# Pooling groups in reverse order, one instruction a level, and group products in four pairs of banks

## The chip, the core and the metric

The kernel runs on one core of a Trainium2 chip. Its engines are TensorE (PE, matmuls into the PSUM banks), VectorE (DVE), ScalarE (ACT), GpSimd (POOL) and SyncE (SP), which issues most transfers. Each has its own queue of instructions and works through it in order; they wait for each other on semaphores. The metric is the time of one execution on the device in microseconds (us).

## The reference

A two-layer decoder trunk runs once for a prompt of 512 positions and for 8 samples of 4 positions, which share the weights. Each layer is a half-step SwiGLU feed-forward, a token mixer and another half-step feed-forward, each followed by a residual and a LayerNorm. The change lies in the mixer of the first layer, a causal pooling:

```
u = x @ w_in                                         # 1024 -> 1024
u_ext = concatenate([prefix, u])                     # 15 rows of history ahead of each sample
for g, w in enumerate((2, 4, 8, 16)):                # four groups of 256 features
    win_sum = sum of u_ext over the last w positions
    pooled = win_sum / min(pos + 1, w) - u           # of the group's 256 features
    outs.append(pooled @ w_grp[g])                   # 256 -> 256
z = concatenate(outs) * scale
mix = z @ w_out                                      # 1024 -> 1024
```

The last 15 rows of `u_ext` are an output too.

## The kernel before

All 544 positions (512 + 32) lie along the columns, and the features on the 128 partitions, in 8 chunks (`DC`). Two halves of 272 columns fill a pair of PSUM banks; there are four pairs, `ps[0]` to `ps[3]`. For precision each matmul of float32 data is made three times: both operands are split into a rounded part ("hi", made by ScalarE) and a remainder ("lo", made by VectorE), and hi x hi, hi x lo and lo x hi are added in PSUM. One output chunk of a 1024 x 1024 weight, a unit below, is 8 steps x 3 x 2 = 48 matmuls of 272 columns. Weights come through two raw tiles (s = 0, 1), which SP loads in order; `round_hi` (ACT, L1352) and `round_lo` (DVE, L1803) make their parts in `whi[s]`/`wlo[s]`. The semaphores `lo_made[s]` and `w_used[s]` say that a weight is ready and that it has been used.

The pooling mixer has three stages, "pin" (x @ w_in), "pgrp" (the group products) and "pout" (z @ w_out):

- **pin.** The first four of the 8 units are made half by half while the LayerNorm ahead still runs (`first_units`, L799): units (0, s) go into `ps[0]` and `ps[1]`, units (1, s) into `ps[2]` and `ps[3]`. Their second half waits step by step for the low part of the normed stream (`x_ready`, L2151). The other four units (i = 2, 3) go into `ps[0]` and `ps[1]`, each after ScalarE has copied the chunk before out of that pair (`u_evac`, L1638 to L1643).
- **windows.** For each chunk c VectorE puts the 15 history rows into the extended chunk `ue[s]` (L2224), then adds level by level (w = 1, 2, 4, 8): a level is one instruction over the prompt's columns (L2230) and one over the samples' (L2232). Group g = c // 2 has g + 1 levels, so the chunks come with 1, 1, 2, 2, 3, 3, 4, 4 levels. Four short instructions make the pooled difference (L2242 to L2249); ScalarE rounds it (L1620), and VectorE makes its low part inside the next chunk's window (L2206, `pooled`). Weight parts of the units to come are made in between.
- **pgrp.** TensorE turns `utail` (the last 47 columns of all chunks) and then makes 8 group products of 12 matmuls, in turn in `ps[0]` and `ps[1]` (L1036 to L1044). A product waits for its two pooled chunks and until the product two before has been read. ScalarE scales each into `zf` and rounds that (L1667, L1669); VectorE makes the low part (L2259, `z_ready`). ScalarE's next read of the same `zf` waits for that.
- **pout.** The first output unit waits for all eight low parts (L1045). Behind it the residual and the next LayerNorm follow, and the feed-forward of up1a.

Of the kernel before, what the change touches and what calls it, by code (L numbers as in the profile page):

```python
# [30 lines left out]
P = 128  # L31
# [58 lines left out]

RBASE = {n: 10 * j for j, n in enumerate(RES)}
# [92 lines left out]
def build(nc, A, O):  # L184
# [9 lines left out]
    with ctx:  # L194
# [320 lines left out]
        def unit_source(stage, s, i):  # L515
# [8 lines left out]
            w = {"pin": w_pin, "pout": w_pout, "kv": w_kv, "q": w_q, "wo": w_o}[stage]  # L524
# [221 lines left out]
        def _(pe):  # L746
            def products(out, s, kt, hi, lo, first=True, last=True, each=None, at=0):


                for k in range(kt):  # L750
                    if each:
                        each(k)
                    for n, (w, a) in enumerate(((whi[s], hi), (whi[s], lo), (wlo[s], hi))):
                        for j in range(2):
                            m = nc.tensor.matmul(out[:, j, 0:HALF], w[:, at + k, :], a(k)[:, j * HALF:(j + 1) * HALF],  # L755
                                                 start=first and k == 0 and n == 0,
                                                 stop=last and k == kt - 1 and n == 2)
                return m
# [40 lines left out]
            def first_units(stage, normed):  # L799
# [25 lines left out]
                for u, k in ((0, 0), (1, 0), (0, 1), (1, 1), (0, 2), (1, 2), (0, 3), (0, 4), (0, 5), (0, 6), (0, 7),  # L825
                             (1, 3), (1, 4), (1, 5), (1, 6), (1, 7)):
# [156 lines left out]
            def linear(stage, hi, lo, evac, normed=None, each=None):  # L983
# [3 lines left out]
                def turn(i, first):  # L987
                    for s in range(2):
# [3 lines left out]
                        products(ps[s], s, KT[stage], hi, lo, each=each if first and s == 0 else None) \  # L992
# [36 lines left out]
            linear("pin", stream_x, stream_xl, lambda s, i: pe.wait_ge(u_evac, 2 * i - 1 + s), "down0b")  # L1029

            pe.wait_ge(u_evac, DC)
            for c in range(DC):
                m = nc.tensor.transpose(pc[0:PAD + SAMP, c // 4, (c % 4) * P:(c % 4 + 1) * P], utail[:, c, :], ident[:])
            m.then_inc(utail_t, 1)

            for g in range(4):  # L1036
                for s in range(2):
                    if g == 0:
                        pe.wait_ge(lo_made[s], USED["pgrp"] + 1)
                    pe.wait_ge(pooled, 2 * g + 2)  # L1040
                    if g >= 1:
                        pe.wait_ge(z_scaled, 2 * g - 1 + s)
                    m = products(ps[s], s, 2, lambda k: phi[:, 2 * g + k, :], lambda k: plo[:, 2 * g + k, :], at=2 * g)
                    m.then_inc(w_used[s] if g == 3 else z_done, 1)  # L1044
            pe.wait_ge(z_ready, DC)  # L1045
            linear("pout", lambda k: zhi[:, k, :], lambda k: zlo[:, k, :],
                   lambda s, i: pe.wait_ge(res_made, RBASE["pout"] + 2 * i - 1 + s))
# [301 lines left out]
        def _(act):  # L1349
# [268 lines left out]
            def pool_hi(c):  # L1618
                act.wait_ge(diff_made, c + 1)
                nc.scalar.activation(phi[:, c, :], (accs, accq)[c % 2], ACT.Copy).then_inc(diff_hi_made, 1)  # L1620

            def pin(i, nxt, j):
                for s in range(2):
                    c = 2 * i + s
                    out = ps[2 + s] if i == 1 else ps[s]
                    if i == 0 and s == 0:
                        round_hi(nxt, 0, j)
                        round_hi(nxt, 1, j)
                    if i > 0:
                        round_hi(nxt, s, j)  # L1630
                    act.wait_ge(w_used[s], USED["pin"] + i + 1)
                    if i >= 1:
                        act.wait_ge(diff_made, 2 * (i - 1) + s + 1)
                        pool_hi(c - 2)
                    else:
                        act.wait_ge(consts_made, 4)
                    samples = ue[s][:, 16 + SEQ:].rearrange("p (b t) -> p b t", t=20)[:, :, 16:20]
                    nc.scalar.activation(ue[s][:, 16:16 + HALF], out[:, 0, 0:HALF], ACT.Copy)  # L1638
                    nc.scalar.activation(ue[s][:, 16 + HALF:16 + SEQ], out[:, 1, 0:SEQ - HALF], ACT.Copy)
                    nc.scalar.activation(samples, out[:, 1, SEQ - HALF:HALF].rearrange("p (b t) -> p b t", t=4),  # L1640
                                         ACT.Copy)
                    nc.scalar.activation(utail[:, c, :], out[:, 1, HALF - PAD - SAMP:HALF], ACT.Copy) \
                        .then_inc(u_evac, 1)  # L1643

            for i in range(UNITS["pin"] - 1):
                pin(i, *coming("pin", i))
                if i >= 1:
                    add_shift("pin", i - 1)
            pin(UNITS["pin"] - 1, "pgrp", 0)
            pool_hi(DC - 2)  # L1650
            pool_hi(DC - 1)
# [4 lines left out]


            for c in range(DC):
                s = c % 2
                if c < DC - 2:  # L1660
                    act.wait_ge(z_done, c + 1)
                else:
                    act.wait_ge(w_used[s], USED["pgrp"] + 1)
# [938 lines left out]
```

## Time and profile before

| | us |
|---|---|
| median of 3 runs | 2211.88 |
| lowest and highest of them | 2200.86 to 2218.66 |
| profiled execution, span from first to last instruction (the page gives no other time for it) | 2210.1 |
| TensorE busy in it | 2089.8 (95%) |
| VectorE, ScalarE, GpSimd busy | 1423.9, 871.4, 227.9 |

The page gives the busy time of each engine and the groups of instructions that cost most. What the rows further down add is an order in time: the timeline of one engine, with the idle time ahead of an instruction and the instruction that ended it, the chain of waits (the work that ended last, followed back from the end), and the busy time of all engines in chosen stretches, with the clock that TensorE was granted (1.00 is 2.4 GHz, 0.50 is 1.2 GHz). The pooling mixer lies from about 425 to 547 us of the span.

### The profile page before, as it was taken

To read this page: it belongs to the slowest core of one execution; us is meant where nothing else is said; L and a number is where in the kernel's file an instruction comes from. 1 tells how busy PE (TensorE), PEld (TensorE's weight loads), DVE (VectorE), ACT (ScalarE), POOL (GpSimd) and SP (SyncE) were. 2 spreads that over 40 slices of the span, in tenths; PEclk is the share of its full clock that TensorE was granted. 3 is DMA by queue.
4 is the path that set the end of the run, shared out by engine and by line. 5 is a ranking of instruction groups with operands and counts; after the bars stand their busy time and mean duration, and the time that the engine had idled before them with its cause. 6 is when DMAs were issued, how large, how long until landed. Compare 5 with 4: busy or idle time off the path is not lost.

```text
span 2210.1 us, 43553 instructions
## 1 busy us (share of the span) xinstructions
PE 2089.8 (95%) x16575; PEld 2016.3 (91%) x16575; DVE 1423.9 (64%) x2388; ACT 871.4 (39%) x1529; POOL 227.9 (10%) x265
## 2 busy tenths in 40 slices
PE   7999999989899999999999999999978789999998
PEld 7999999989899999999999999988866588999997
DVE  3483795674786498378639836266746377838955
ACT  3342453353543255254415524222234345514533
POOL 0000002304100000410000031111012140000022
PEclk9999999999999999999999999999989899999998
DMA  4242433222233233324423333656576422333331
GB/s 140 64 134 84 124 116 107 78 61 77 66 98 102 78 97 94 91 64 147 124 88 96 102 88 108 203 181 224 187 252 219 137 77 86 93 89 95 95 102 54
DMA packets 381501, 249.80 MB, mean 113 GB/s; under 512 B 10422, under 2 KB 363038, under 8 KB 381326
## 3 DMA queue, kind: packets, MB, share of 16 engines
q1 hardware_dynamic: 371271, 210.00, 32.0%
q0 software_dynamic: 10096, 37.94, 5.0%
q8 instruction: 93, 1.52, 0.3%
q14 instruction: 41, 0.34, 0.1%
HBM read 230.63 MB, written 22.35 MB: 114 GB/s over the span
## 4 chain that ended last, share of the span: by engine, by line
PE 73%; DVE 11%; DMA 7%; issue 4%; ACT 3%; SPq 1%; POOL 1%; DVEq 0%; ACTq 0%; POOLq 0%
PE pair L755 33%; PE pair L884 27%; PE pair L794 5%; DMA t_w_raw<-in_attn_w_kv 4%; PE pair L1012 2%; DMA t_w_raw<-in_ffn_w 2%; DVE t_w_seven L1938 2%; PE pair L1238 1%; DVE t_w_sum L1933 1%; PE pair L767 1%; DVE t_w_lo L1816 1%; ACT t_w_hi L1367 1%; DVE t_u_sum L2230 1%; DVE t_stream L2144 1%; DVE t_work L2136 1%
## 5 line engine op out<-in xcount | busy, mean ns | idle before, releaser
L884 PE MATMUL pair<-t_x_diff_hi,t_w_seven 128*128 128x272 f32 x1960 | 409.9, 289 | 0.0
L1816 DVE TENSOR_TENSOR t_w_lo<-t_w_raw,t_w_hi 128x1024 fp32r<-128x1024 f32 (+2 forms) x152 | 232.8, 1532 | 203.3 <-ACT t_w_hi L1367 198.6
L1367 ACT ACTIVATE t_w_hi<-t_w_raw 128x1024 fp32r<-128x1024 f32 (+2 forms) x152 | 177.2, 1170 | 462.8 <-PE pair L755 383.7
L884 PEld LDWEIGHTS pair<-t_x_diff_hi,t_w_seven 128*128 128x128 f32 x1960 | 320.3, 188 | 0.0
L755 PE MATMUL pair<-t_h_lo,t_w_hi 128*128 128x272 f32 x1232 | 254.8, 288 | 0.0
L755 PE MATMUL pair<-t_h_hi,t_w_lo 128*128 128x272 f32 x1232 | 254.6, 288 | 0.0
L755 PE MATMUL pair<-t_h_hi,t_w_hi 128*128 128x272 f32 x1232 | 254.5, 288 | 0.0
L884 PE MATMUL pair<-t_x_hi,t_w_seven 128*128 128x272 f32 x1120 | 240.7, 294 | 10.8 <-DVE t_c L1942 9.5
L884 PE MATMUL pair<-t_x_diff_lo,t_w_seven 128*128 128x272 f32 x840 | 241.7, 288 | 0.0
L884 PEld LDWEIGHTS pair<-t_x_hi,t_w_seven 128*128 128x128 f32 x1120 | 184.5, 188 | 23.1 <-issue 12.4
L755 PEld LDWEIGHTS pair<-t_h_hi,t_w_lo 128*128 128x128 f32 x1232 | 193.2, 188 | 0.0
L755 PEld LDWEIGHTS pair<-t_h_hi,t_w_hi 128*128 128x128 f32 x1232 | 193.2, 188 | 0.0
L755 PEld LDWEIGHTS pair<-t_h_lo,t_w_hi 128*128 128x128 f32 x1232 | 193.0, 188 | 0.0
L1438 ACT ACTIVATE t_w_seven<-t_w_sum 128x512 fp32r<-128x512 f32 x210 | 124.6, 622 | 113.7 <-PE pair L884 78.6
L884 PE MATMUL pair<-t_x_lo,t_w_seven 128*128 128x272 f32 x560 | 161.5, 288 | 0.0
L884 PEld LDWEIGHTS pair<-t_x_diff_lo,t_w_seven 128*128 128x128 f32 x840 | 158.4, 189 | 0.0
L2455 POOL MEMSET t_work<- 128x544 f32 x6 | 3.3, 555 | 1374.0 <-DVE t_stream L2086 1374.0
L1938 DVE TENSOR_TENSOR t_w_seven<-t_w_sum,t_w_seven 128x512 fp32r<-128x512 f32 x210 | 143.2, 682 | 0.2
L1438 ACT ACTIVATE t_s_hi<-t_w_sum 128x512 fp32r<-128x512 f32 x70 | 44.3, 633 | 241.5 <-DVE t_w_sum L1933 229.7
L755 PE MATMUL pair<-t_x_hi,t_w_hi 128*128 128x272 f32 x576 | 123.8, 297 | 15.1 <-DVE t_w_lo L1816 10.4
L755 PE MATMUL pair<-t_x_lo,t_w_hi 128*128 128x272 f32 x576 | 123.0, 296 | 0.0
L755 PE MATMUL pair<-t_x_hi,t_w_lo 128*128 128x272 f32 x576 | 122.3, 294 | 0.0
(320 smaller groups left out, 4898.1 us busy)
## 6 DMA issues: line engine op xcount, KB each, us to landing
t_w_raw<-in_ffn_w SPq DMA_DIRECT2D x280, 256.0 KB, 3.1
t_w_raw<-in_ffn_w SPq DMA_DIRECT2D x64, 704.0 KB, 4.6
t_w_raw<-in_ffn_w SPq DMA_DIRECT2D x36, 512.0 KB, 3.8
t_cached<-in_cache_kv_w POOLq DMA_DIRECT2D x16, 1024.0 KB, 9.3
t_cached_v<-in_cache_kv_w POOLq DMA_DIRECT2D x16, 1024.0 KB, 10.8
t_w_raw<-in_attn_w_kv SPq DMA_DIRECT2D x24, 512.0 KB, 8.2
t_w_raw<-in_attn_w_q SPq DMA_DIRECT2D x12, 512.0 KB, 3.8
scratch_bias_rows<-scratch_bias_row SPq DMA_DIRECT2D x12, 384.0 KB
```

Of the source, the lines that this page charges most:

```text
L755: m = nc.tensor.matmul(out[:, j, 0:HALF], w[:, at + k, :], a(k)[:, j * HALF:(j + 1) * HALF], start=first and k == 0 and n == 0, stop=last ...
L767: return nc.tensor.matmul(out[:, j, 0:HALF], invd[:], a[:, hcols(j)], start=first, stop=not first)
L794: m = nc.tensor.matmul(ps[2 * u + s][:, j, 0:HALF], w[:, k, :], a[:, k, hcols(j)], start=k == 0 and n == 0, stop=k == DC - 1 and n == 2)
L884: m = nc.tensor.matmul(out[:, 0:HALF], w[:, k, :], b, start=start and k == 0 and j == 0, stop=k == 3 and j == 2, skip_group_check=not start)
L1012: m = nc.tensor.matmul(ps[s][:, j, 0:HALF], w[:, k, :], a(k)[:, hcols(j)], start=k == 0 and n == 0, stop=k == KT[stage] - 1 and n == 2)
L1238: m = nc.tensor.matmul(pd[32 * n:32 * n + 32, 0, :], p_b[:, n, t, :], v_c0[n] if t == 0 else v_c[n // 2][:, 4 * (n % 2) + t - 1, :], start ...
L1367: nc.scalar.activation(whi[s][:, 0:KT[stage], :], raw[s][:, 0:KT[stage], :], ACT.Copy) \
L1438: nc.scalar.activation(seven_hi[n][:], src, ACT.Copy).then_inc(seven_hi_made, 1)
L1816: nc.vector.tensor_tensor(wlo[s][:, 0:k, :], raw[s][:, 0:k, :], whi[s][:, 0:k, :].bitcast(F32), ALU.subtract).then_inc(lo_made[s], 1)
L1933: nc.vector.tensor_tensor(w_sum[m][:], a, b, op).then_inc(w_sum_made, 1)
L1938: nc.vector.tensor_tensor(seven_lo[n][:], src, seven_hi[n][:].bitcast(F32), ALU.subtract) \
L2136: step.add(nc.vector.reciprocal(rstd[:, hcols(j)], rstd[:, hcols(j)]))
```

## The change

The chunks go through pin and the windows in reverse: position o stands for chunk `chunk_of(o)`, 6, 7, 4, 5, 2, 3, 0, 1, so the four-level windows come first, and SP reads the columns of w_in in that order. The half-made units are finished one after the other, not interleaved. Units 2 go into `ps[0]`/`ps[1]` and units 3 into `ps[2]`/`ps[3]`. A level is one instruction over the prompt's and the samples' columns together; ScalarE copies the history rows, ahead of the chunk's other copies, and GpSimd fills `ue` with zeros beforehand. The 8 group products go round the four pairs of banks, in the order of `Z_ORDER` = (6, 4, 7, 5, 2, 3, 0, 1). ScalarE scales and rounds a product in one instruction from PSUM, and VectorE makes its low part from PSUM as well; `zf` is gone. The first output unit takes its eight steps in `Z_ORDER`, each as its low part is there, and turns `utail` ahead of its last step.

```diff
+def chunk_of(o):
+    return 2 * (3 - o // 2) + o % 2
+Z_ORDER = (6, 4, 7, 5, 2, 3, 0, 1)
...
+            if stage == "pin":
+                return w_pin[:, :, bass.ds(-2 * P * i + (6 + s) * P, P)]
...
+                if stage == "pin":
+                    second_half = [(u, k) for u in range(2) for k in range(DC)]
+                for u, k in second_half:
                     pe.wait_ge(x_ready, ready + DC + k + 1)
...
-            linear("pin", stream_x, stream_xl, lambda s, i: pe.wait_ge(u_evac, 2 * i - 1 + s), "down0b")
...
+            first_units("pin", "down0b")
+            for i in (2, 3):
+                for n in range(2):
+                    pe.wait_ge(lo_made[n], USED["pin"] + i + 1)
+                    pe.wait_ge(u_evac, n + 1 if i == 2 else n + 3)
+                    products(ps[n if i == 2 else 2 + n], n, DC, stream_x, stream_xl).then_inc(w_used[n], 1)
+            def grouped(n, g, w):
+                pe.wait_ge(pooled, 2 * (3 - g) + 2)
+                return products(ps[n % 4], w, 2, lambda k: phi[:, 2 * g + k, :], lambda k: plo[:, 2 * g + k, :], at=2 * g)
+            for n, g in ((0, 3), (1, 2)):
+                if n == 0:
+                    pe.wait_ge(lo_made[0], USED["pgrp"] + 1)
+                pe.wait_ge(u_evac, 5 + n)
+                grouped(n, g, 0).then_inc(z_done, 1)
+            for n, g in ((2, 3), (3, 2)):
+                if n == 2:
+                    pe.wait_ge(lo_made[1], USED["pgrp"] + 1)
+                pe.wait_ge(u_evac, 5 + n)
+                grouped(n, g, 1).then_inc(z_done, 1)
+            for n in (4, 5):
+                pe.wait_ge(z_ready, n - 3)
+                grouped(n, 1, n - 4).then_inc(z_done, 1)
+            for n in (6, 7):
+                pe.wait_ge(z_ready, n - 3)
+                grouped(n, 0, n - 6).then_inc(w_used[n - 6], 1)
+            def pout_first(k):
+                if k == Z_ORDER[0]:
+                    pe.wait_ge(z_ready, 5)
+                pe.wait_ge(z_ready, Z_ORDER.index(k) + 1)
+                if k == Z_ORDER[-1]:
...
             linear("pout", lambda k: zhi[:, k, :], lambda k: zlo[:, k, :],
+                   lambda s, i: pe.wait_ge(res_made, RBASE["pout"] + 2 * i - 1 + s), each=pout_first, order=Z_ORDER)
...
+            def evacuated(o):
+                i, n, c = o // 2, o % 2, chunk_of(o)
+                out = ps[2 + n] if i % 2 else ps[n]
+                samples = ue[n][:, 16 + SEQ:].rearrange("p (b t) -> p b t", t=20)
+                if o >= 2:
+                    act.wait_ge(diff_made, o - 1)
+                elif o == 0:
+                    act.wait_ge(consts_made, 4)
+                nc.scalar.activation(samples[:, :, 1:16], hist[:, c, :].rearrange("p (b t) -> p b t", t=PAD), ACT.Copy)
+                act.wait_ge(w_used[n], USED["pin"] + i + 1)
...
+            def scaled_hi(n):
+                c = Z_ORDER[n]
+                if n < 6:
+                    act.wait_ge(z_done, n + 1)
+                else:
+                    act.wait_ge(w_used[n - 6], USED["pgrp"] + 1)
+                nc.scalar.activation(split(zhi[:, c, :]), halves(ps[n % 4]), ACT.Copy, scale=par[:, PS + c:PS + c + 1]) \
+                    .then_inc(z_scaled, 1)
...
+            round_hi("pin", 1, 3)
+            pool_hi(2)
+            evacuated(4)
+            pool_hi(3)
+            evacuated(5)
+            round_hi("pgrp", 0, 0)
+            pool_hi(4)
+            evacuated(6)
+            round_hi("pgrp", 1, 0)
+            pool_hi(5)
+            evacuated(7)
...
+            for n in range(4, 7):
+                scaled_hi(n)
+            round_hi("pout", 0, 0)
+            scaled_hi(7)
+            round_hi("pout", 1, 0)
...
+            def window(o):
+                n, g = o % 2, chunk_of(o) // 2
...
+                for level in range(g + 1):
+                    dst = us[level % 2]
+                    step.add(nc.vector.tensor_tensor(dst[:, 2 * w - 1:end], src[:, 2 * w - 1:end], src[:, w - 1:end - w],
+                                                     ALU.add))
+                    if o == 0 and level == 0:
+                        round_lo("pin", 0, 2)
...
+                if o in (2, 3):
+                    round_lo("pin", o - 2, 3)
+                if o in (5, 6):
+                    round_lo("pgrp", o - 5, 0)
+                if o:
+                    pool_lo(o - 1)
...
+                if o == 0:
+                    round_lo("pin", 1, 2)
+            def scaled_lo(n):
+                c = Z_ORDER[n]
+                dve.wait_ge(z_scaled, n + 1)
+                nc.vector.scalar_tensor_tensor(out=split(zlo[:, c, :]), in0=halves(ps[n % 4]),
+                                               scalar=par[:, PS + c:PS + c + 1], in1=split(zhi[:, c, :]).bitcast(F32),
+                                               op0=ALU.mult, op1=ALU.subtract).then_inc(z_ready, 1)
...
             centre("down0b")
...
+            for s in range(2):
+                nc.gpsimd.memset(ue[s][:], 0.0).then_inc(consts_made, 1)
```

Three places of the instruction order show what moves. In these rows a number behind a name tells buffers apart (`pair0` is `ps[0]`), and in brackets stand the semaphores that an instruction waits for.

VectorE at the start of the windows, before:

```order
L1816 TENSOR_TENSOR t_w_lo0<-t_w_raw0,t_w_hi0 128x1024 [waits hi_made0,consts_in]
L1816 TENSOR_TENSOR t_w_lo1<-t_w_raw1,t_w_hi1 128x1024 [waits hi_made1]
L2224 COPY t_u_ext0<-t_history 128x8x15 [waits state_evacuated]
L2230 TENSOR_TENSOR t_u_sum0<-t_u_ext0 128x527 [waits u_evacuated,dve_step]
L2232 TENSOR_TENSOR t_u_sum0<-t_u_ext0 128x8x18
L2242 TENSOR_TENSOR t_u_sum1<-t_u_sum0,t_inv_count 128x16 [waits dve_step]
L2243 SCALAR_TENSOR_TENSOR t_work<-t_u_sum0,t_u_ext0 128x496
L2245 SCALAR_TENSOR_TENSOR t_work<-t_u_sum0,t_u_ext0 128x32
L2249 TENSOR_TENSOR t_work<-t_u_sum1,t_u_ext0 128x16 [waits dve_step]
```

and now:

```order
L2265 TENSOR_TENSOR t_u_sum0<-t_u_ext0 128x687 [waits u_evacuated,consts_in]
L1862 TENSOR_TENSOR t_w_lo0<-t_w_raw0,t_w_hi0 128x1024 [waits hi_made0]
L2265 TENSOR_TENSOR t_u_sum1<-t_u_sum0 128x685 [waits dve_step]
L2265 TENSOR_TENSOR t_u_sum0<-t_u_sum1 128x681 [waits dve_step]
L2265 TENSOR_TENSOR t_u_sum1<-t_u_sum0 128x673 [waits dve_step]
L2281 TENSOR_TENSOR t_u_sum0<-t_u_sum1,t_inv_count 128x16 [waits dve_step]
L2282 SCALAR_TENSOR_TENSOR t_work<-t_u_sum1,t_u_ext0 128x496
L2284 SCALAR_TENSOR_TENSOR t_work<-t_u_sum1,t_u_ext0 128x32
L2288 TENSOR_TENSOR t_work<-t_u_sum0,t_u_ext0 128x16 [waits dve_step]
L1862 TENSOR_TENSOR t_w_lo1<-t_w_raw1,t_w_hi1 128x1024 [waits hi_made1]
```

The first chunk's first level stands ahead of both weight parts instead of behind them, it is one instruction, and the copy of the history has left VectorE; the first chunk has four levels instead of one.

VectorE between the last windows and the output weights, before:

```order
L2249 TENSOR_TENSOR t_work<-t_u_sum0,t_u_ext1 128x16 [waits dve_step]
L2206 TENSOR_TENSOR t_pool_lo<-t_work,t_pool_hi 128x544 [waits pool_hi_made]
L2259 TENSOR_TENSOR t_z_lo<-t_elementwise,t_z_hi 128x544 [waits z_scaled] x7
L1816 TENSOR_TENSOR t_w_lo0<-t_w_raw0,t_w_hi0 128x1024 [waits hi_made0]
L2259 TENSOR_TENSOR t_z_lo<-t_elementwise,t_z_hi 128x544 [waits z_scaled]
L1816 TENSOR_TENSOR t_w_lo1<-t_w_raw1,t_w_hi1 128x1024 [waits hi_made1]
```

and now:

```order
L2295 SCALAR_TENSOR_TENSOR t_z_lo<-pair0,t_params,t_z_hi 128x544 [waits z_scaled]
L2295 SCALAR_TENSOR_TENSOR t_z_lo<-pair1,t_params,t_z_hi 128x544 [waits z_scaled]
L2265 TENSOR_TENSOR t_u_sum0<-t_u_ext1 128x687 [waits u_evacuated,pool_diff_made]
...
L2288 TENSOR_TENSOR t_work<-t_u_sum1,t_u_ext1 128x16 [waits dve_step]
L2295 SCALAR_TENSOR_TENSOR t_z_lo<-pair2,t_params,t_z_hi 128x544 [waits z_scaled]
L2251 TENSOR_TENSOR t_pool_lo<-t_work,t_pool_hi 128x544 [waits pool_hi_made]
L2295 SCALAR_TENSOR_TENSOR t_z_lo<-pair3,t_params,t_z_hi 128x544 [waits z_scaled]
...
L1862 TENSOR_TENSOR t_w_lo0<-t_w_raw0,t_w_hi0 128x1024 [waits hi_made0]
L2295 SCALAR_TENSOR_TENSOR t_z_lo<-pair2,t_params,t_z_hi 128x544 [waits z_scaled]
...
L1862 TENSOR_TENSOR t_w_lo1<-t_w_raw1,t_w_hi1 128x1024 [waits hi_made1]
```

Three of the scaled low parts (`t_z_lo`) moved ahead of the last low pooled part (`t_pool_lo`), and all eight read a pair of banks instead of `zf` in SBUF (`t_elementwise`).

TensorE, the first matmul of each group product and what stands next to it, before:

```order
L1033 MATMUL pair2<-t_ident,t_u_tail 47x128 [waits u_evacuated]
L755 MATMUL pair0<-t_pool_hi,t_w_hi0 128x272 [waits pooled,lo_made0]
...
L755 MATMUL pair1<-t_pool_hi,t_w_hi1 128x272 [waits pooled,lo_made1]
...
L755 MATMUL pair0<-t_pool_hi,t_w_hi0 128x272 [waits z_scaled,pooled]
...
L755 MATMUL pair1<-t_pool_hi,t_w_hi1 128x272 [waits z_scaled,pooled]
...
L755 MATMUL pair0<-t_z_hi,t_w_hi0 128x272 [waits lo_made0,z_parts_ready]
```

and now:

```order
L762 MATMUL pair0<-t_pool_hi,t_w_hi0 128x272 [waits pooled,u_evacuated,lo_made0]
...
L762 MATMUL pair1<-t_pool_hi,t_w_hi0 128x272 [waits pooled,u_evacuated]
...
L762 MATMUL pair2<-t_pool_hi,t_w_hi1 128x272 [waits pooled,u_evacuated,lo_made1]
...
L762 MATMUL pair3<-t_pool_hi,t_w_hi1 128x272 [waits pooled,u_evacuated]
...
L762 MATMUL pair0<-t_pool_hi,t_w_hi0 128x272 [waits pooled,z_parts_ready]
...
L762 MATMUL pair1<-t_pool_hi,t_w_hi1 128x272 [waits pooled,z_parts_ready]
...
L762 MATMUL pair0<-t_z_hi,t_w_hi0 128x272 [waits z_parts_ready,lo_made0]
...
L762 MATMUL pair0<-t_z_hi,t_w_hi0 128x272 [waits z_parts_ready]
...
L1075 MATMUL pair2<-t_ident,t_u_tail 47x128 [waits z_parts_ready]
```

The third to eighth product waited for `z_scaled` of the pair that it writes, two products before it; now the first four wait for pooled chunks and banks alone, and only the last four for a low part (`z_parts_ready`). The turning of `utail` moved from ahead of the group products into the first output unit.

## Rows read from the trace of the kernel before

**Rows 1.** The page, busy time of TensorE: us, share of the span, instructions.

```profile
PE 2089.8 (95%) x16575; PEld 2016.3 (91%) x16575; DVE 1423.9 (64%) x2388; ACT 871.4 (39%) x1529; POOL 227.9 (10%) x265
```

**Rows 2.** Busy time in stretches: us, us long, busy us (x) of each engine, PEclk, DMA.

```profile
454.00:482.00 28.00, 24.67 (x197) 24.24 (x196) 27.35 (x70) 17.51 (x43) 0.00 (x0) 1.00 0.27 76
482.00:491.00 9.00, 2.35 (x17) 1.92 (x15) 6.62 (x17) 3.24 (x7) 1.10 (x2) 0.85 0.20 59
```

**Rows 3.** Chain of waits, pooling stage: start, us, what.

```profile
487.99 0.66 ACT t_pool_hi L1620
...
491.04 6.61 PE pair L755 x36
```

**Rows 4.** VectorE in time, a window of four levels: start, us, instruction, [idle before it and its releaser].

```profile
476.22 0.21 DVE L2224 COPY t_u_ext<-t_history 128x120 f32<-128x120 f32 x1
476.47 0.71 DVE L2230 TENSOR_TENSOR t_u_sum<-t_u_ext 128x527 f32<-128x527 f32 x1
477.09 0.30 DVE L2232 TENSOR_TENSOR t_u_sum<-t_u_ext 128x144 f32<-128x144 f32 x1
...
479.28 0.69 DVE L2230 TENSOR_TENSOR t_u_sum<-t_u_sum 128x513 f32<-128x513 f32 x1
...
479.99 0.72 DVE L2206 TENSOR_TENSOR t_pool_lo<-t_work,t_pool_hi 128x544 fp32r<-128x544 f32 x1
480.62 0.17 DVE L2242 TENSOR_TENSOR t_u_sum<-t_u_sum,t_inv_count 128x16 f32<-128x16 f32 x1
...
481.48 1.22 DVE L1816 TENSOR_TENSOR t_w_lo<-t_w_raw,t_w_hi 128x1024 fp32r<-128x1024 f32 x1
```

**Rows 5.** VectorE in time, the ends of its chain.

```profile
444.93 0.50 DVE L2151 SCALAR_TENSOR_TENSOR t_x_lo<-t_stream,t_params,t_x_hi 128x272 fp32r<-128x272 f32 x1 [0.18 <-ACT t_x_hi L1570]
...
449.52 2.36 DVE L1816 TENSOR_TENSOR t_w_lo<-t_w_raw,t_w_hi 128x1024 fp32r<-128x1024 f32 x2 [4.05 <-ACT t_w_hi L1367]
...
488.68 0.72 DVE L2206 TENSOR_TENSOR t_pool_lo<-t_work,t_pool_hi 128x544 fp32r<-128x544 f32 x1 [0.72 <-ACT t_pool_hi L1620]
```

**Rows 6.** TensorE in time: second half of the projection, two pauses, two output products.

```profile
440.21 0.29 PE L794 MATMUL pair<-t_x_hi,t_w_hi 128*128 128x272 f32 x1
...
480.00 1.07 PE L1033 MATMUL pair<-t_ident,t_u_tail 128*47 128x128 f32 x8 [2.48 <-ACT t_u_tail L1642]
...
505.47 0.82 PE L755 MATMUL pair<-t_z_hi,t_w_hi 128*128 128x272 f32 x2 [2.66 <-DVE t_z_lo L2259]
...
513.07 0.41 PE L755 MATMUL pair<-t_z_hi,t_w_hi 128*128 128x272 f32 x2
```

**Rows 7.** Chain of waits, a stage at the full clock.

```profile
167.31 66.38 PE pair L755 x528
```

**Rows 8.** ScalarE in time: the first copy out of PSUM, the second chunk's.

```profile
450.27 0.38 ACT L1638 ACTIVATE t_u_ext<-pair 128x272 f32<-128x272 f32 x1
...
450.96 0.42 ACT L1638 ACTIVATE t_u_ext<-pair 128x272 f32<-128x272 f32 x1
```

**Rows 9.** Groups by line and form: xcount, busy us, mean ns, idle before.

```profile
L1367 ACT ACTIVATE t_w_hi<-t_w_raw 128x1024 fp32r<-128x1024 f32 x8 | 8.3, 1054 | 10.8 <-PE pair L755 7.4 <-PE pair L794 3.5
L2259 DVE TENSOR_TENSOR t_z_lo<-t_elementwise,t_z_hi 128x544 fp32r<-128x544 f32 x8 | 5.8, 725 | 8.8 <-ACT t_z_hi L1669 8.7
L1667 ACT ACTIVATE t_elementwise<-pair,t_params 128x544 f32<-128x544 f32 x8 | 5.7, 708 | 3.2 <-PE pair L755 3.0
```

**Rows 10.** VectorE in time, the same operands from PSUM.

```profile
513.26 0.73 DVE L2086 SCALAR_TENSOR_TENSOR t_stream<-pair,t_stream 128x544 f32<-128x544 f32 x1 [6.40 <-PE pair L755]
```

**Rows 11.** Busy time and PEclk in single microseconds.

```profile
506.00:507.00 1.00, 1.00 (x7) 1.00 (x6) 0.86 (x1) 0.00 (x0) 0.00 (x0) 0.50 0.92 272
509.00:510.00 1.00, 1.00 (x10) 1.00 (x10) 0.00 (x0) 0.00 (x0) 0.00 (x0) 1.00 1.00 302
```

**Rows 12.** GpSimd in time: a fill of 544 columns.

```profile
514.05 0.55 POOL L2455 MEMSET t_work<- 128x544 f32 x1 [22.86 <-DVE t_stream L2086]
```

**Rows 13.** Transfers, 440 to 520 us: issues, KB each, median us to landing.

```profile
t_w_raw<-in_pool_w_out SPq DMA_DIRECT2D x5, 512.0 KB, 4.1
```

More of the change, by code:

```diff
@@ L746, in _, with products @@
         def _(pe):
-            def products(out, s, kt, hi, lo, first=True, last=True, each=None, at=0):
-                for k in range(kt):
+            def products(out, s, kt, hi, lo, each=None, at=0, order=None):
+                order = order or range(kt)
+                for k in order:
                     if each:
@@ L755, in products @@
                             m = nc.tensor.matmul(out[:, j, 0:HALF], w[:, at + k, :], a(k)[:, j * HALF:(j + 1) * HALF],
-                                                 start=first and k == 0 and n == 0,
-                                                 stop=last and k == kt - 1 and n == 2)
+                                                 start=k == order[0] and n == 0,
+                                                 stop=k == order[-1] and n == 2)
                 return m
@@ L981, in down, with linear @@
                 linear(stage, lambda k: hhi[:, k, :], lambda k: hlo[:, k, :], evac, each=each)
-            def linear(stage, hi, lo, evac, normed=None, each=None):
+            def linear(stage, hi, lo, evac, normed=None, each=None, order=None):
                 base = USED[stage]
@@ L991, in turn @@
                             evac(s, reused(stage, i))
-                        products(ps[s], s, KT[stage], hi, lo, each=each if first and s == 0 else None) \
+                        products(ps[s], s, KT[stage], hi, lo, each=each if first and s == 0 else None, order=order) \
                             .then_inc(w_used[s], 1)
@@ L1615, in _ @@
             norm("down0b", 0)
[L1618 to L1643, printed above, removed]
@@ new lines, in scaled_lo @@
+            def scaled_lo(n):
[4 more added lines that the diff above has]
+                                               op0=ALU.mult, op1=ALU.subtract).then_inc(z_ready, 1)
+            dve.wait_ge(consts_in, 32)
+            for o in range(7):
+                window(o)
@@ L2264, in _ @@
+            scaled_lo(0)
+            scaled_lo(1)
+            window(7)
+            scaled_lo(2)
+            pool_lo(7)
+            for n in range(3, 6):
+                scaled_lo(n)
+            round_lo("pout", 0, 0)
+            scaled_lo(6)
+            scaled_lo(7)
+            round_lo("pout", 1, 0)
             residual_pair("pout")
```

155 lines of the change are left out of this document (60 added, 95 removed).

## The prediction

> **What bounds the kernel now.** I read the page first: TensorE is busy for 95% of the span [rows 1], so a change in one stage is worth the TensorE time that this stage leaves empty, and no more. The busy time by stretches then shows where it is empty: from 454 to 482 us 3.3 of 28.0 us, and from 482 to 491 us, where the pooling windows end, 6.65 of 9.0 [rows 2]. The chain of waits says who is waited for there: ScalarE's high part of the last pooled chunk at 487.99, and only from 491.04 on the group products that follow [rows 3]. VectorE in time shows the reason: four-level windows end the stage, and its chain of one instruction after another runs from 449.52 to 488.68 + 0.72 = 489.40 [rows 4, 5]. TensorE in time: it waited 2.48 us for the last `u_tail`, and 2.66 us before the first output product at 505.47 [rows 6]. So the stage is bound by VectorE until 489.4, then by the ping-pong of six group products on two banks, product, scale, part, next product, for 505.47 - 489.40 = 16.07 us.
>
> **The prices.** A full-rate matmul of 272 columns costs 66.38 / 528 = 0.1257 us [rows 7]; a unit of 48 is 6.03, a group product of 12 is 1.51. On VectorE I count from start to start, which is the duration less 0.09 where nothing is waited for (476.47 to 477.09 for 0.71), and the duration plus about 0.04 where the next needs the result (476.22 + 0.21 to 476.47) [rows 4]. The new level instruction of up to 687 columns is not in the trace. Between 144 columns (0.30) and 527 (0.71) a column costs 0.00107 us, so 687 cost 0.71 + 160 x 0.00107 = 0.88 [rows 4]: 0.92 with a wait behind it, 0.79 without. Its bounds: 0.71, a row with fewer columns, and 1.01, the two that it replaces (0.71 + 0.30). I take 0.88, nearest to the larger row. The four instructions that close a window cost 481.48 - 480.62 = 0.86, a low pooled part 0.63, a weight's low part 1.22 - 0.08 = 1.14 [rows 4].
>
> The scaled low part, a SCALAR_TENSOR_TENSOR of 544 columns that reads PSUM, stands in the trace as a residual: 0.73, against 0.725 for the subtraction from SBUF that it replaces [rows 9, 10]. I take 0.64 from start to start, as 0.63 above. The Trainium skill, VectorE: DVE Perf Modes, section on the TRN2 errata, prices the fixed part of a VectorE instruction at 120 cycles from PSUM and 58 from SBUF, at 0.96 GHz. By that each would cost 0.065 us more, and the three ahead of the last pooled part 0.2 us together, for a gain of 15.6 instead of the 15.8 below; the rows do not show it.
>
> **The change, part by part.** *Head.* The first unit's second half now runs by itself: eight steps of six matmuls from 440.21 [rows 6], each 0.75 and held by a low part of the stream, the last of which ends at 444.93 + 0.50 = 445.43 [rows 5]. Unit 0 ends at about 446.2; before, three steps of unit 1 stood between, and 11 x 0.75 give 448.5. ScalarE copies the chunk at once (four copies, 450.96 - 450.27 = 0.69 [rows 8]) and rounds the next weight behind it, not ahead of it, so VectorE's first level starts at about 446.9. Unit 1 still ends at 452.25, since the number of matmuls is the same.
>
> *VectorE from there to the last low pooled part.* Windows without the parts: with four levels 3 x 0.92 + 0.79 + 0.87 = 4.42; three 3.50, two 2.58, one 1.66; two of each are 24.3. Eight pooled parts 5.0, six weight parts 6.8, three scaled parts 1.9: 38.1 in all, and I add 0.9 for some 15 hops between engines. It ends at 446.9 + 39.0 = 485.9, 3.5 us before 489.4. Of these 3.5, 2.6 are the early start, 2.0 the eight history copies (476.47 - 476.22 = 0.25 each [rows 4]) that go to ScalarE, some 0.8 the merged levels and a shorter last wait; the three scaled parts, now ahead of the end, take 1.9 back.
>
> *TensorE beside it.* Units 2 to 5 (four of 48) run from 452.25 to 458.3, 464.3, 470.3 and 476.4, if their weights' low parts are there. In VectorE's order these end at 449.0, 453.8, 462.7 and 468.1: the least margin is 1.6 us, at the third (464.3 - 462.7). The two group weights end at 475.9 and 479.4. Four products into four pairs of banks run from 476.4 to 482.5 and wait for nothing but the second weight; two more, behind the low parts of the first two, to 485.5; the last two wait for the last pooled part and run from 485.95 to 488.97.
>
> *Tail.* Behind 485.9 there is now: two products 3.02, with the seventh's high part (0.71) and the first output weight's rounding (1.05) and low part (1.22) behind the first of them [rows 4, 9]: 487.5 + 0.6 + 1.05 + 1.25 = 490.4. TensorE starts the output products at 490.45, after a pause of 1.5 us, instead of at 505.47: 15.0 us earlier, 3.5 of it before the last pooled part and 11.5 behind.
>
> *First output unit.* It took 513.07 - 505.47 = 7.60 us [rows 6], 1.57 above 6.03, since the granted clock was 0.50 there [rows 11]. It was low after a pause of 2.66 us and had stayed at 1.00 through one of 2.48 [rows 2, 6, 11], so I expect it to stay after 1.5. The `u_tail` transposes now stand inside this unit: eight, 0.83 us. Net gain 0.74. **Sum: 15.0 + 0.74 = 15.8 us at the end of that unit.** Behind it TensorE's order is as before.
>
> *At nothing:* the history copies on ScalarE, bounded by 0.25 each (VectorE's), stand ahead of chunks for which VectorE is 1.7 us late or more, except the first two, where ScalarE waits for TensorE; without that cover they cost 8 x 0.25 = 2.0. GpSimd's two fills of 688 columns (0.55 for 544 [rows 12], so 0.7 each) end some 5 us before the first copy. One wide copy less per scaled chunk on ScalarE is inside the 11.5. Transfers: 4.1 us from issue to landing [rows 13]; the output weights are issued when the group weights' low parts are made, at 475.9 and 479.4, and wanted at 488.1 and 489.7, so they are not late. SP's queue keeps its order; only the columns that it reads are reversed. GpSimd's two stores of `u_tok` and ScalarE's two copies for them move into the first output unit, where both engines wait for TensorE.
>
> **Against the runs.** The sum is made on the profiled execution, of which the page gives the span, 2210.1, and no other time. The median 2211.88 lies 1.8 above it. I take the difference over to the median: 2211.88 - 15.8 = **2196 us**, 0.7% faster. More is not to be had: from 452.25 the stage holds 4 x 6.03 + 8 x 1.51 + 0.83 + 6.03 = 43.1 us of matmuls, which would end at 495.3, and 513.07 - 495.3 = 17.8 is the most.
>
> **Rivals.** *Ring waits, 12%.* TensorE waits for a weight's low part, VectorE for ScalarE's high part, ScalarE at the head of its queue for TensorE to let go of the old weight. Margins are 1.6 us at the third late weight and about 0.5 and 0 at the group weights; if each of four such turns comes 2 us late, 8 us are lost: 2204. For it: level instructions at their upper bound make VectorE 20 x 0.13 = 2.6 late. Against: VectorE waited 0.72 us in its chain before [rows 5].
>
> *The clock falls, slower, 3%.* The products now run in batches of 1.5 us on four pairs of banks with small pauses, then pause 1.5 us. If the clock went to its lower level, 1.2 GHz, at 476 and stayed there through the output products, 12.1 + 288 x 0.1257 = 48.3 us of matmuls would double: 2211.88 - 15.8 + 48.3 = 2244. It decides from 15.8 us of doubled work on. Against it: 1.00 through a pause of 2.48 us, and the return to 1.00 inside the first output unit [rows 2, 6, 11]. The Trainium skill, TensorE: Matmul & The Clock Gate, section on psum-queue depth-cycling, says that such cycling through banks, with TensorE idle for a moment between groups, makes the clock fall and rise again. In this stage of the trace it fell only behind pauses of 2.66 us and more.
>
> *Gained and given back, 5%.* A wait behind the stage eats the gain, 2212: the one transfer that could is an output weight, with 3 us to spare.
>
> The forecast has 80%. It covers gains of 10 (levels at 1.01, the clock low for the first output unit, 1 us of hops) to 17.8: 2194 to 2202. The three runs of before lie 11.0 below and 6.8 above their median, so a median of after may be read 10 us off. **Range 2183 to 2208**, which takes in the ring. Within 1% means 22 us, about what a measurement of this kernel can tell from no change; no case gains that much, so "faster by over 1%" is left to the scatter, about one in five of the forecast: 0.17. Slower by over 1% is the clock's case: 0.03. The rest is 0.80.
>
> **What would show it.** In the profile after: the first level at about 447, the last low pooled part ending near 486, no pause of TensorE over 2 us from 452 to the output products, these beginning near 490, and the granted clock 1.00 throughout. It is wrong if TensorE pauses inside the four late units, if the level rows are over 1.0 us, or if a wait of that size comes up behind the first output unit.

## The result: 0.8% shorter, the stage as forecast

The changed kernel took 2192.36 us (median of four runs, 2189.58 to 2195.15) beside 2212.68 (2200.86 to 2218.66) of the kernel before: ratio 0.9921, interval 0.9898 to 0.9945. The forecast was 2196, range 2183 to 2208; the time lies in it, 3.6 us below the forecast, and 0.8% shorter by the ratio, inside the 1% that held 0.80 of the chances. The profiled execution after has a span of 2193.5 us and took 2195.15.

The page after, TensorE's busy time, answers to [rows 1]: the work is the same, and 3.0 us less is counted (the second execution of before counts 2086.8 too).

```profile
PE 2086.8 (95%) x16575; PEld 2014.1 (92%) x16575; DVE 1421.7 (65%) x2358; ACT 867.4 (40%) x1529; POOL 228.8 (10%) x267
```

Busy time in stretches after, in the columns of [rows 2]:

```profile
454.00:482.00 28.00, 28.00 (x225) 27.86 (x224) 27.62 (x55) 15.53 (x41) 0.00 (x0) 1.00 0.27 77
482.00:491.00 9.00, 7.07 (x55) 6.67 (x54) 6.58 (x9) 4.48 (x7) 0.00 (x0) 1.00 0.18 55
```

The 3.33 us that TensorE left empty from 454 to 482 are gone, 6.65 us of the next nine are now 1.93, and the granted clock is 1.00 in both. TensorE's waits over the stage (444 to 506 us; in total, times, longest), the kernel before first:

```profile
PE pair L755 <- ACT t_z_hi L1669: 6.5, 1, 6.5
PE pair L755 <- DVE t_z_lo L2259: 2.7, 1, 2.7
PE pair L1033 <- ACT t_u_tail L1642: 2.5, 1, 2.5
PE pair L755 <- DVE t_w_lo L1816: 1.0, 2, 0.8
```

and after:

```profile
PE pair L762 <- DVE t_w_lo L1862: 1.5, 1, 1.5
PE pair L762 <- DVE t_pool_lo L2251: 0.4, 1, 0.4
```

The chain of waits after, the pooling stage (start, us, what), answers to [rows 3, 5, 6]:

```profile
426.19 16.77 PE pair L801 x132
...
443.93 0.88 DVE t_u_sum L2265
...
482.07 0.73 DVE t_pool_lo L2251
482.94 1.76 PE pair L762 x12
...
485.33 1.06 ACT t_w_hi L1400
486.42 1.24 DVE t_w_lo L1862
487.70 5.51 PE pair L762 x42
493.21 0.87 PE pair L1075 x8
```

It reads as forecast: VectorE's levels to the last low pooled part, two group products, the first output weight, the output products. But both executions have to be put on one start. Ahead of the change, where the code is equal, the second execution already led: the products of the projection's second unit begin in the chain at 429.43 before and at 426.19 after. Their first product stands 0.37 us ahead of that; TensorE in time, before and after:

```profile
429.06 0.49 PE L794 MATMUL pair<-t_x_hi,t_w_hi 128*128 128x272 f32 x1
```

```profile
425.82 0.49 PE L801 MATMUL pair<-t_x_hi,t_w_hi 128*128 128x272 f32 x1
```

**D** is the time from that first product to the first output product (505.47 before [rows 6], 487.70 after): **76.41 us before, 61.88 after, 14.53 less**, where 15.0 were forecast.

### The profile page after: what moved, and what is told of

It reads as the page before. It is cut to its first block, busy times and chain, and to the rows that moved or that the text cites. A ratio compares the mean times of both kernels' runs of the same rounds, so it can differ in the third digit from the quotient of the medians.

```text
span 2193.5 us, 43507 instructions
## 1 busy us (share of the span) xinstructions
PE 2086.8 (95%) x16575; PEld 2014.1 (92%) x16575; DVE 1421.7 (65%) x2358; ACT 867.4 (40%) x1529; POOL 228.8 (10%) x267
## 4 chain that ended last, share of the span: by engine, by line
PE 73%; DVE 11%; DMA 6%; issue 4%; ACT 3%; SPq 1%; POOL 1%; DVEq 0%; ACTq 0%; POOLq 0%
PE pair L762 33%; PE pair L894 27%; PE pair L801 5%; DMA t_w_raw<-in_attn_w_kv 3%; PE pair L1022 2%; DMA t_w_raw<-in_ffn_w 2%; DVE t_w_seven L1984 2%; DVE t_w_lo L1862 1%; PE pair L1271 1%; DVE t_w_sum L1979 1%; PE pair L774 1%; DVE t_u_sum L2265 1%; ACT t_w_hi L1400 1%; DVE t_stream L2190 1%; DVE t_u L1988 1%
## 5 line engine op out<-in xcount | busy, mean ns | idle before, releaser
L894 PE MATMUL pair<-t_x_hi,t_w_seven 128*128 128x272 f32 x1120 | 240.7, 295 | 11.2 <-DVE t_c L1988 9.9
```

The lines of the kernel that those rows point to most:

```text
L894: m = nc.tensor.matmul(out[:, 0:HALF], w[:, k, :], b, start=start and k == 0 and j == 0, stop=k == 3 and j == 2, skip_group_check=not start)
```

## The experiments

All are read by D, since single runs of this kernel spread by over 10 us and D by much less. "Pooled" is the end of the last low pooled part, counted from the chain's start of that unit (429.43 before, 426.19 after).

| kernel | D, us | pooled | what is different |
|---|---|---|---|
| before, twice | 76.41, 77.05 | 59.97, 60.02 | |
| change, twice | 61.88, 61.93 | 56.60, 56.66 | |
| head alone | 72.64 | 55.37 | tail as before |
| tail alone | 69.24 | 63.74 | head as before, natural order |
| u1 | 64.00 | 58.73 | interleaved first units |
| u3 | 64.21 | 58.95 | two instructions a level, copies on VectorE |
| u4 | 62.92 | 56.86 | parts through SBUF |
| u2 | 67.30 | 59.15 | two pairs of banks |
| u6 | 65.82 | 55.37 | scaled parts behind the windows |
| u5 | 69.24 | 62.66 | natural order |
| n1 | 65.72 | 59.14 | natural order, weights' parts later |
| b1 | 61.37 | 56.64 | a shorter pause ahead of pout |

**The two kernels once more (no edit).**

> The kernel before, once more, for its scatter. D is the time from the first product of pin's second unit (it stands right behind the sums of the norm) to the first product of pout: 76.41 us in the first profile of before, 61.88 in the first of the changed kernel. Theory (the stage's gain of 14.5 us belongs to the code, the 3.2 us by which the changed kernel led ahead of the stage do not): D is 76.4 +- 0.4 again, while the start of that first product may lie anywhere in 425 to 430. Rival (part of the 14.5 is the scatter of one execution): D is off by 1 us or more.

> The changed kernel, once more. Theory: D is 61.9 +- 0.4; the norm sums behind pout take 3.4 us or 6.2 us, whichever clock the execution meets, since nothing there was changed; total about 20 us below before with an interval that holds 15. Rival (the change itself lowers the clock behind pout): they take 6.2 us again here and in every variant that starts pout early, and 3.4 only with the tail of before.

D came out 77.05 and 61.93. The change repeats; before missed its 0.4 us, and stayed short of the rival's 1. Of the 0.64 us, 0.59 lie in the three group products behind TensorE's longest pause: their 36 matmuls took 7.20 us, 6.61 the first time [rows 3], and 4.53 (36 x 0.1257) would be the full clock. The unit that D counts from began anywhere from 423.99 to 430.17 us in the traces of this study, so the lead of 3.2 us was scatter. The change again: 2193.11 us beside 2210.94, ratio 0.9917 (0.9899 to 0.9934). The norm sums behind pout separate the two executions of the same code. Chain of waits, first profile after:

```profile
544.23 1.05 PE pair L801 x3
545.28 1.81 PE pair L774 x4
...
550.41 19.20 PE pair L801 x153
```

and the second one:

```profile
545.35 0.65 PE pair L801 x3
546.00 0.92 PE pair L774 x4
...
548.75 19.20 PE pair L801 x153
```

From the start of these three matmuls to the chain that follows it is 6.18 us in the one, at a granted clock of 0.54 in the mean, and 3.40 in the other, at 1.00. Over the variants it fell on either kind: 5.07 us with the tail of before (head alone), 3.40 in b1, which has the tail of the change. So the rival that the change lowers the clock there falls. In the first profile it gave back 2.78 of the stage's gain.

**Head alone, tail alone.** Tail alone has the natural order, of which this is the core, and the edits of u1 and u3 below:

```diff
 def chunk_of(o):
-    return 2 * (3 - o // 2) + o % 2
+    return o
-Z_ORDER = (6, 4, 7, 5, 2, 3, 0, 1)
+Z_ORDER = (0, 2, 1, 3, 4, 5, 6, 7)
```

> The tail alone: chunks in natural order, the first two units' second halves interleaved as before, two instructions a level and the history copies on VectorE; group products on four pairs of banks and parts straight from PSUM, scaled parts between the windows, as in the change. Theory (head and tail add up, the reverse order by itself gives nothing): 2.3 us lost by the interleaving and 2.4 by VectorE's longer chain, D = 66.6 (65.5 to 68), total about 10 us below before. Rival (the reverse order, long windows first, is what lets six of eight products run before the last pooled part): D = 70 or more.

Head alone has the edits of u2, u4 and u6 below, together.

> The head alone: reverse order, the first unit finished by itself, one instruction a level, history copies on ScalarE as in the change; group products on two pairs of banks, scaled through SBUF by two ScalarE instructions, all scaled parts behind the last pooled part, as before. Theory: the last low pooled part ends 2.2 us earlier than in the change (no scaled part ahead of it), the ring of before's 16.1 us follows: D = 70 (69 to 72), total about 6 us below before. Rival (the reverse order alone brings most): D below 66. Rival (the head is worth nothing without the tail): D above 74.

Tail alone: D = 69.24, between theory and rival, so missed; 2204.72 us, ratio 0.9975 (0.9959 to 0.9991). Head alone: D = 72.64, just over the range; 2206.12 us, ratio 0.9973 (0.9957 to 0.9989). Apart they gain 3.8 to 4.4 and 7.2 to 7.8 us of D, 10.9 to 12.2 of 14.5 to 15.1: the parts don't simply add up. Head alone shows the old ring; TensorE's waits over the stage:

```profile
PE pair L762 <- issue: 6.6, 1, 6.6
PE pair L762 <- DVE t_w_lo L1862: 2.4, 1, 2.4
PE pair L762 <- DVE t_z_lo L2295: 1.0, 4, 0.3
```

**One part undone: the order.** u5 has the natural order and nothing else: the two lines above, the unit's columns from the front, and in the group products

```diff
+                g = 3 - g
-                pe.wait_ge(pooled, 2 * (3 - g) + 2)
+                pe.wait_ge(pooled, 2 * g + 2)
```

> The change with the chunks in natural order (short windows first), all else as in the change. D is 61.9 in the change; the tail alone had 69.2, of which 2.3 + 2.4 were expected of its interleaving and its longer VectorE chain, and 2.6 stay over. Theory (the 2.6 are the order: with short windows first VectorE waits between chunks, and the long ones end the stage): D = 64.5 (63.5 to 66). Rival (the order is worth nothing, the two undone head parts cost more than their sum): D = 62 (61.5 to 62.7).

D = 69.24, 7.4 us above the change and the same as in tail alone: theory and rival both missed. 2201.38 us, ratio 0.9958 (0.9936 to 0.998) to before. VectorE in time shows where it stands still:

```profile
456.87 1.22 DVE L1863 TENSOR_TENSOR t_w_lo<-t_w_raw,t_w_hi 128x1024 fp32r<-128x1024 f32 x1 [3.34 <-ACT t_w_hi L1401]
...
462.87 1.22 DVE L1863 TENSOR_TENSOR t_w_lo<-t_w_raw,t_w_hi 128x1024 fp32r<-128x1024 f32 x1 [1.47 <-ACT t_w_hi L1401]
```

The low part of the next weight stands in the middle of a window in VectorE's order; ScalarE can round that weight only when TensorE has let go of the old one, every 6.0 us. Behind a short window VectorE is there early and waits, and the rest of the window with it. With the long windows first it is never early: in the change VectorE shows no such wait from its first level (443.93) to 486.42. With the natural order the head parts, 4.4 us in the change, are worth little. For these two weights VectorE waits 4.8 us in u5 and 2.0 in tail alone, and the last pooled part comes 1.1 us earlier in u5. That D is the same looks like chance: the next product met a lower clock in u5, which took the 1.1 us back. The chain of tail alone, then of u5:

```profile
488.24 1.99 PE pair L762 x12
```

```profile
489.35 3.07 PE pair L762 x12
```

n1 is u5 with the parts of pin's last two weights one window later, and their roundings on ScalarE one chunk later:

```diff
-                if o in (2, 3):
-                    round_lo("pin", o - 2, 3)
+                if o in (3, 4):
+                    round_lo("pin", o - 3, 3)
```

> The change in natural order again, with the roundings of pin's last two weights and their low parts one window later on ScalarE and VectorE. In natural order as first run (D = 69.2, 7.3 us above the change) VectorE stood still 3.34 and 1.47 us in the windows of chunks 2 and 3, behind low parts of weights that ScalarE could round only when TensorE had let go of the old ones. Theory (the reverse order gains because long windows cover those weights): the two pauses go or shrink below 1 us, the last low pooled part ends 59 to 60 us after the second unit's products begin instead of 62.7, D = 64.8 (64 to 66.3). Rival (the order matters at the end: long windows last hold the stage up whatever stands between the first): D = 68 or more.

D = 65.72, pooled 59.14, both in the ranges: the first two waits for a weight's part are gone, one of 0.56 us is left, beside 0.96 and 0.62 for the high parts of the first two pooled chunks. 2198.26 us, ratio 0.9937 (0.992 to 0.9953). So 3.5 of the order's 7.4 us were those waits. The other 3.8 are 2.5 by which the last pooled part is still later and 1.3 of clock: TensorE paused 3.1 us for it, and the next product (12 matmuls) then took 3.07 us, against 1.76 in the change. The first row is the chain of n1, the second its busy time and clock (0.50):

```profile
486.66 3.07 PE pair L762 x12
```

```profile
486.60:489.70 3.10, 3.04 (x13) 3.07 (x14) 1.99 (x3) 0.36 (x1) 0.00 (x0) 0.50 0.00 0
```

**One part undone: the head.** u1 leaves out two lines:

```diff
-                if stage == "pin":
-                    second_half = [(u, k) for u in range(2) for k in range(DC)]
```

> The change with the second halves of pin's first two units interleaved as before. Theory (VectorE's chain is the bound from the first chunk on, so its later start shows in full): the first level 2.3 us later, D = 64.2 (63.8 to 64.6). Rival (VectorE waits for chunks later on anyway, the start is hidden): D = 62 (61.5 to 62.5).

u3 copies the history on VectorE, not on ScalarE, and adds each level in two instructions:

```diff
+                step.add(nc.vector.tensor_copy(tail(e)[:, :, 1:16],
+                                               hist[:, chunk_of(o), :].rearrange("p (b t) -> p b t", t=PAD)))
...
-                    step.add(nc.vector.tensor_tensor(dst[:, 2 * w - 1:end], src[:, 2 * w - 1:end], src[:, w - 1:end - w],
-                                                     ALU.add))
+                    nc.vector.tensor_tensor(dst[:, 2 * w - 1:16 + SEQ], src[:, 2 * w - 1:16 + SEQ],
+                                            src[:, w - 1:16 + SEQ - w], ALU.add)
+                    step.add(nc.vector.tensor_tensor(tail(dst)[:, :, 2 * w:20], tail(src)[:, :, 2 * w:20],
+                                                     tail(src)[:, :, w:20 - w], ALU.add))
```

> The change with two instructions a level and the history copies on VectorE. Theory (20 merged levels bring at most 0.8, eight copies of 0.25 us 2.0, all of it on VectorE's chain): D = 64.3 (63.7 to 64.9). Rival (both are hidden by chunks that come late): D = 62 (61.5 to 62.5).

D = 64.00 and 64.21, both in the range: 2.1 us for the start of the chain, 2.3 for its length, all of it on the path. (One run each, 2195.87 and 2194.67 us, which alone would say nothing.)

**One part undone: the tail.** In u2 `n % 4` becomes `n % 2` for the products and both parts, and the waits of products 2 and 3, of 4 to 7, and of pout become

```diff
-                pe.wait_ge(u_evac, 5 + n)
+                pe.wait_ge(z_ready, n - 1)
...
-                pe.wait_ge(z_ready, n - 3)
+                pe.wait_ge(z_ready, n - 1)
...
-                    pe.wait_ge(z_ready, 5)
+                    pe.wait_ge(z_ready, 7)
```

> The change with the group products on two pairs of banks (each product waits until the part of the product two earlier is read, and pout until both pairs are free); scaled parts between the windows and straight from PSUM stay. Theory (each turn of the ring costs a product, a high and a low part, some 3 us, but most turns lie beside windows): D = 65 (64 to 67). Rival (the four pairs carry the tail's gain): D = 68 or more. Rival (they are worth nothing): D below 62.5.

u4 scales into SBUF and rounds from there; the low part is a subtraction from SBUF:

```diff
...
+                step.add(nc.scalar.activation(split(zf[:]), halves(ps[n % 4]), ACT.Copy, scale=par[:, PS + c:PS + c + 1]))
+                act.wait_ge(act_step, step.value())
+                nc.scalar.activation(zhi[:, c, :], zf[:], ACT.Copy).then_inc(z_scaled, 1)
```

> The change with the scaled chunks going through SBUF: two ScalarE instructions of 0.70 and 0.66 us each instead of one, VectorE subtracting from SBUF. Theory (ScalarE has idle time between the windows, so only the parts behind the last pooled part show): D = 63.1 (62.6 to 64.5); VectorE's low part takes 0.72 instead of 0.72 to 0.77 us. Rival (parts straight from PSUM carry the tail's gain): D = 66 or more.

u6 on ScalarE; on VectorE the low parts move alike:

```diff
-            scaled_hi(0)
-            scaled_hi(1)
             pool_hi(6)
-            scaled_hi(2)
-            scaled_hi(3)
             pool_hi(7)
-            for n in range(4, 7):
+            for n in range(7):
                 scaled_hi(n)
```

> The change with all scaled parts behind the last pooled part, as before (four pairs of banks and parts straight from PSUM stay). Theory: the last low pooled part ends 2.2 us earlier (three scaled parts fewer ahead of it), but products 5 to 8 wait for the parts one after another: D = 63 (62.4 to 64). Rival (the place of the parts among the windows is what the tail's gain is made of): D = 66 or more.

u2: D = 67.30, 0.3 over the range, 0.7 short of the rival's. u4: 62.92, in the range. u6: 65.82, missed, 0.2 short of the rival's. Both misses have the clock in them, which their expectations left out. u2's chain:

```profile
480.98 4.79 PE pair L762 x24
...
488.56 3.29 PE pair L762 x24
...
495.59 4.47 PE pair L762 x34
```

and its busy time and clock:

```profile
478.00:481.00 3.00, 0.82 (x8) 0.63 (x6) 3.00 (x8) 2.29 (x6) 0.00 (x0) 1.00 0.39 114
481.00:483.00 2.00, 2.00 (x11) 2.00 (x12) 2.00 (x5) 0.00 (x0) 0.00 (x0) 0.64 0.47 138
```

The ring makes TensorE pause 2.2 us, and the two products behind it take 4.79 us instead of 3.02. Then ScalarE, held by the scaled part of the second of them, comes late to the last pooled part (pooled 2.5 us later). In u6 the pooled part comes 1.2 us earlier, but TensorE pauses 2.8 us ahead of the fifth product, and three products take 6.33 us instead of 4.53 (chain of u6):

```profile
482.15 6.33 PE pair L762 x36
```

**A shorter pause ahead of pout.** In the change ScalarE scales the seventh chunk and rounds the first output weight after it, while TensorE waits 1.5 us. b1 turns that round, and the `u_tail` transposes go ahead of pout, into `ps[1]`:

```diff
-            for n in range(4, 7):
-                scaled_hi(n)
+            scaled_hi(4)
+            scaled_hi(5)
             round_hi("pout", 0, 0)
+            scaled_hi(6)
             scaled_hi(7)
```

> The change, with pout's first weight rounded ahead of the seventh scaled part, and the tail transposes moved from the first output unit into the pause ahead of it (into the second pair of banks). Theory (the pause of 1.5 us ahead of pout is ScalarE's order and nothing else): D = 61.3 (60.9 to 61.5), the first output unit 0.87 us shorter, 1.5 us gained at its end; total 1.5 us below the change, less than a comparison of this kernel can show. Rival (the pause is filled, but a later wait comes up, for the seventh and eighth scaled parts or the second weight): the unit's end is not earlier by more than 0.5 us.

D = 61.37, in the range; TensorE waits in all 0.4 us in the stage (its waits, 444 to 506 us):

```profile
PE pair L762 <- DVE t_pool_lo L2255: 0.4, 1, 0.4
```

From the first output product to the end of the norm sums behind pout b1 takes 59.04 us, against 59.94 in the second profile of the change, so 1.4 us are gained in all, as expected. The total, 2194.27 us and ratio 0.9936 (0.9913 to 0.9958) to before, can't show that: b1 is better in the profile, and not shown to be faster than the change.

## Why the prediction was right, step by step

- **Head, 3.5 us.** Pooled came 3.37 us earlier (59.97 to 56.60). Its terms: 2.6 for the early start, 2.1 by u1; 2.8 for copies and levels, 2.3 by u3; 1.9 given back for three scaled parts ahead of the end, 1.2 by u6. That is 3.2 of the 3.37. Only two of the three parts cost time: the third runs while ScalarE rounds the last pooled chunk, where VectorE waits 0.72 us in u6. A merged level took 0.88 us as priced. The price of the scaled low part was low: from start to start two of them took 1.39 / 2 = 0.70, where 0.64 was taken. VectorE in time, after: two scaled parts, then for comparison one pooled part of the same size from SBUF and an instruction of the same kind from SBUF:

```profile
477.60 1.47 DVE L2295 SCALAR_TENSOR_TENSOR t_z_lo<-pair,t_params,t_z_hi 128x544 fp32r<-128x544 f32 x2
...
479.77 0.72 DVE L2251 TENSOR_TENSOR t_pool_lo<-t_work,t_pool_hi 128x544 fp32r<-128x544 f32 x1
...
480.49 0.66 DVE L2282 SCALAR_TENSOR_TENSOR t_work<-t_u_sum,t_u_ext 128x496 f32<-128x496 f32 x1
```

  Behind the last of these rows the next instruction starts at 481.08, so 496 columns took 0.59 from start to start, and 544 would take 0.64 (an estimate with 0.00107 a column); the kind of instruction is not what makes 0.70. The Trainium skill, VectorE: DVE Perf Modes, section on the TRN2 errata, would have 0.065 us more for a source in PSUM; the trace agrees, with 0.06.
- **TensorE beside it.** No pause from 454 to 482, as forecast, and the waits of TensorE shown with the result name none of the late weights.
- **Tail, 11.5 us.** From the last low pooled part to pout it was 16.07 us before and is 487.70 - 482.80 = 4.90: 11.2 less. The pause ahead of pout is 1.51, forecast 1.5. Not all of the 16.07 was the ping-pong, as the prediction has it: 2.1 us (6.61 less 4.53 [rows 3]; 2.7 in the second execution) were the low clock of three products behind the pause of 6.5 us, which went with the pause; the size of the step stays the same by it. And the step took the gain as one sum and said nothing of what carries it. Undone alone, the order costs 7.4 us, the two pairs 5.4, the late parts 3.9, the way through SBUF 1.0; with the head's 4.4 that is 22 for a gain of 14.5. Each of the larger ones opens a pause of TensorE of over 2 us and then pays for the clock as well, so the price of one part depends on the others.
- **First output unit, 0.74.** The clock stayed at 1.00, and the transposes took 0.87 inside it. From the first output product to the end of the norm sums behind pout it was 60.48 us before (565.95 - 505.47) and 59.94 in the second profile of the change: 0.54.
- **Sum, 15.8.** From the second unit's chain start to the end of the norm sums behind pout it is 565.95 - 429.43 = 136.52 us before and 550.41 - 426.19 = 124.22 after, or 121.44 without the 2.78 of the low clock: 15.1 less. In the second pair it is 137.22 and 121.50: 15.7 less. The medians differ by 20.3 and, in the larger comparison, 17.8 us. The other 2 to 5 us need not be the change's, and that the median lies 3.6 us below the forecast says nothing: ahead of the stage traces differ by 6.2 us, and behind those norm sums by up to 7.4 (1639.8 to 1647.2 us to the end of the span). The interval of the second comparison, 14.6 to 22.3 us, holds the stage's gain. The chain of waits before, both ends of the 136.52 us:

```profile
429.43 18.85 PE pair L794 x150
...
565.95 19.20 PE pair L794 x153
```

- **Rivals.** The ring waits did not come (one wait of 0.4 us). The clock fell in neither profile from 454 us to pout, so the forecast held, but one of its grounds did not: the pause of 2.48 us that had kept 1.00 was followed by 0.50 in the second execution of before, and in tail alone the clock fell behind 1.9 us. That the clock stays up behind 1.5 us rests on the five profiles that have this pause (the change twice, u1, u3, u6). What the first profile gave back behind pout was not a wait, as the third rival has it, but the clock, in one execution of two.

## What to carry to other kernels

Where one engine's fixed order holds both a chain of windows and the parts of weights that another engine frees at its own pace, put the long windows first, or the parts behind work that covers the wait; shortening the chain gives little as long as it waits (here 1.1 of 4.4 us). Read a part's gain with the others in place and again alone: here two halves alone showed 11 to 12 us of 14.5, and the parts undone one by one 22, so neither sum is the gain. Compare a stage between two points in the trace when its gain is near the scatter of whole runs.

## What was not expected of the hardware

The granted clock fell to 0.50 behind some pauses of TensorE and not behind others that were as long. It fell behind pauses of 1.9 and 3.2 us (tail alone), 2.2 (u2), 2.66 and 5.6 to 6.5 (before), 2.8 (u6), 3.1 (u5, n1) and 6.6 (head alone). It stayed at 1.00 behind 1.5 (change), 1.9 (u2), 2.3 (u4), 2.4 (head alone) and, in u5, a pause of 3.0 us ahead of the third group product (u5, busy time and clock in single microseconds):

```profile
477.00:478.00 1.00, 0.00 (x0) 0.00 (x0) 0.96 (x2) 0.97 (x2) 0.00 (x0) 1.00 0.00 1
...
480.00:481.00 1.00, 1.00 (x8) 1.00 (x9) 1.00 (x3) 0.00 (x0) 0.00 (x0) 1.00 0.00 2
```

The same pause met both: 2.48 us ahead of the `u_tail` transposes in before, ended at 480.00 in the first execution [rows 6] and at 476.41 in the second. Busy time and clock behind it, first and second execution:

```profile
480.00:481.00 1.00, 1.00 (x9) 1.00 (x10) 1.00 (x4) 0.00 (x0) 0.00 (x0) 1.00 0.01 2
```

```profile
477.00:478.00 1.00, 1.00 (x7) 0.95 (x6) 1.00 (x6) 0.00 (x0) 0.00 (x0) 0.50 0.07 16
```

The same code behind pout, with the same two pauses of 1.24 us ahead of the norm sums, met the lower clock in one execution and 1.00 in another. The length of the last pause alone does not tell; what does is left open.
